# Differential attention: two units' half panels of queries and keys put behind the logits of one unit

## What is computed

```python
def diff_attention(h, pos, w_qkv, q_gain, k_gain, ..., rel_table, lam_init):
    qkv = h @ w_qkv
    q = rms_norm_2(qkv[..., :qk_w].reshape(b, s, DIFF_HEADS, 2, DIFF_QK_DIM), q_gain)
    k = rms_norm_2(qkv[..., qk_w:2 * qk_w].reshape(b, s, DIFF_HEADS, 2, DIFF_QK_DIM), k_gain)
    v = qkv[..., 2 * qk_w:].reshape(b, s, DIFF_HEADS, DIFF_V_DIM)
    ...
        sc = jnp.einsum('bqhcd,bkhcd->bhcqk', q_blk, k).astype(f32) * scale
        ...
        sc = jnp.where(causal_mask(i, s), sc + bias, NEG_INF)
        a = jax.nn.softmax(sc, axis=-1)
        wts = a[:, :, 0] - lam * a[:, :, 1]
        return jnp.einsum('bhqk,bkhv->bqhv', wts.astype(v.dtype), v)
    ...
    o = rms_norm_2(o, sub_gain) * (1.0 - lam_init)
    return o.reshape(b, s, DIFF_HEADS * DIFF_V_DIM) @ w_o
```

## Time and profile before

| | before |
|---|---|
| median of 3 runs | 2942.85 us (2942.21 to 2944.64) |
| the profiled execution | 2943.78 us |
| its span, first to last instruction | 2942.0 us |
| PE busy | 2830.5 us, 96% of the span |
| DVE busy | 1883.5 us, 64% |
| ACT busy | 1157.5 us, 39% |
| mean granted clock of PE | 0.989 of full speed |
| the loop over units, on PE | about 1468.8 to 1628 us of the span |

### The profile page before, as it was taken

One profiled execution on the slowest core, in us unless ns is written; L12 is line 12 of the kernel. 1 busy time (PEld: TensorE's weight loads), 2 busy tenths in 40 slices (PEclk: granted clock), 3 DMA queues, 4 the chain that ended last, 5 costly groups with the idle time before them and its releaser, 6 DMA issues.

```text
span 2942.0 us, 41954 instructions
## 1 busy us (share of the span) xinstructions
PE 2830.5 (96%) x14930; PEld 2267.2 (77%) x14930; DVE 1883.5 (64%) x3191; ACT 1157.5 (39%) x2228; POOL 726.7 (25%) x831
## 2 busy tenths in 40 slices
PE   8999999998999999999999899999989999999999
PEld 5777866776676899876766699987757767799987
DVE  6775346796345888447466688855755554788745
ACT  2111023333443566014255378711355551378501
POOL 1001003343141587000000078800000000188500
PEclk9999999999999999999999999999999999999999
DMA  4335422211112233322322123343211111233432
GB/s 154 109 105 119 131 92 80 79 65 65 47 50 83 79 102 105 113 90 103 101 85 70 58 86 109 103 131 93 86 43 36 37 37 66 71 101 109 138 98 93
DMA packets 81210, 259.15 MB, mean 88 GB/s; under 512 B 9128, under 2 KB 15656, under 8 KB 80776
## 3 DMA queue, kind: packets, MB, share of 16 engines
q1 hardware_dynamic: 64656, 227.64, 23.8%
q10 hardware_dynamic: 16376, 29.20, 3.4%
HBM read 242.51 MB, written 14.16 MB: 87 GB/s over the span
## 4 chain that ended last, share of the span: by engine, by line
PE 83%; DVE 10%; ACT 4%; issue 2%; POOL 1%; ACTq 0%; DMA 0%; SPq 0%; DVEq 0%
PE ps L327 17%; PE ps L328 16%; PE ps L329 16%; PE ps L1014 6%; PE ps L1015 6%; PE ps L1016 6%; PE ps L4381 1%; DVE w_lo L310 1%; PE ps L4426 1%; PE ps L4402 1%; PE ps L4403 1%; DVE w_hi L301 1%; PE ps L3896 1%; PE ps L1467 1%; PE ps L3156 1%
## 5 line engine op out<-in xcount | busy, mean ns | idle before, releaser
L301 DVE CAST w_hi<-raw 128x1024 fp32r<-128x1024 f32 (+1 forms) x311 | 212.2, 682 | 524.0 <-PE ps L329 492.7
L327 PE MATMUL ps<-xh,w_hi 128*128 128x512 f32 x1200 | 505.4, 421 | 32.1 <-DVE xl L851 12.3
L328 PE MATMUL ps<-xl,w_hi 128*128 128x512 f32 x1200 | 479.3, 399 | 0.0
L329 PE MATMUL ps<-xh,w_lo 128*128 128x512 f32 x1200 | 478.3, 399 | 0.0
L1376 POOL TENSOR_TENSOR w_lo<-raw,w_hi 128x256 fp32r<-128x256 f32 x440 | 337.0, 792 | 135.6 <-ACT w_hi L1067 132.7
L327 PEld LDWEIGHTS ps<-xh,w_hi 128*128 128x128 f32 x1200 | 228.1, 190 | 133.9 <-issue 43.8
L1368 POOL TENSOR_TENSOR raw<-raw 128x256 f32<-128x256 f32 x120 | 93.9, 803 | 952.7 <-DMA raw<-in_conv_up 904.8
L310 DVE TENSOR_TENSOR w_lo<-raw,w_hi 128x1024 fp32r<-128x1024 f32 (+2 forms) x259 | 308.6, 1191 | 12.4
L327 PE MATMUL ps<-ah,w_hi 128*128 128x512 f32 x704 | 278.5, 396 | 0.7 <-DVE w_lo L310 0.7
L329 PE MATMUL ps<-ah,w_lo 128*128 128x512 f32 x704 | 278.3, 395 | 0.0
L328 PE MATMUL ps<-al,w_hi 128*128 128x512 f32 x704 | 278.3, 395 | 0.0
(11 more groups left out here) (494 smaller groups left out, 5742.5 us busy)
## 6 DMA issues: line engine op xcount, KB each, us to landing
raw<-in_ffn_up SPq DMA_DIRECT2D x90, 512.0 KB, 3.5
raw<-in_conv_up SPq DMA_DIRECT2D x88, 512.0 KB, 3.4
raw<-in_ffn_down SPq DMA_DIRECT2D x32, 512.0 KB, 3.7
raw<-in_conv_down SPq DMA_DIRECT2D x32, 512.0 KB, 3.6
raw<-in_merge SPq DMA_DIRECT2D x24, 512.0 KB, 3.5
raw<-in_ple_gate SPq DMA_DIRECT2D x24, 512.0 KB, 3.4
raw<-in_diff SPq DMA_DIRECT2D x24, 512.0 KB, 3.4
raw<-in_mla SPq DMA_DIRECT2D x20, 512.0 KB, 3.4
```

Source lines behind the costliest of these rows:

```text
L301: dve.tensor_copy(self.w_hi[s][:, 0:n], self.raw[r][:, 0:n]).then_inc(self.sem["slot_hi"], 1)
L327: pe.matmul(out, wh, xh, start=start, stop=False)
L328: pe.matmul(out, wh, xl, start=False, stop=False)
L329: return pe.matmul(out, wl, xh, start=False, stop=stop)
```

## The change

Both halves of a panel are projected in the unit in which the first half stood, and the unit of the second half projects nothing. So whole panels of keys stand in the units with b = 0 and whole panels of queries in those with b = 2, behind the logits and the sum of that unit.

```diff
             item, half = self.item_in(u)
-            if item is not None:
-                self.project(pe, item, half)
+            if item is not None and half == 0:
+                self.project(pe, item, 0)
+                self.project(pe, item, 1)
             self.out.beside(pe, u)
```

## The result

The changed kernel takes 2969.98 us in the median of four runs (2968.68 to 2976.45), against 2942.94 us for the kernel before (2942.21 to 2944.64): a ratio of 1.0096, 95% interval 1.0084 to 1.0108. It is slower by 27.0 us; 30 us were forecast. The profiled execution took 2968.89 us, its span is 2967.1 us.

The account below looks back on a forecast made before the run. PE's own work was taken to bound the loop. Queries 16.8, keys 3.8 and clock 9.5 us sum to 30 us, set on the 2942.85 us median: 2973 us forecast, range 2961 to 2983.

Parts of the forecast that it names:

- The bound: In the loop, PE's own work sets the pace; any standstill adds time, and under 4 us could be won back.
- Queries, b = 3: At head borders, mask to next query sum stays 5.69 us; PE idles for the moved half, 6 x 2.8 = 16.8 us.
- Keys, b = 1: After b = 1's mask, the key sum waits for ACT's square: 2.3 us over six heads, 1.5 in the first, 3.8 together.
- The wait of 0.4 us: PE's wait before the key sum of b = 2, about 0.4 us in each of six heads.
- DVE's rounding ahead of the row minimum: In b = 2 the row minimum stands behind earlier rounding; PE's 5.6 us query panel covers this, so no cost.
- The clock: Idle of 3.3 us at five borders drops the clock: 1.9 us each, 9.5 us in all, bounds 0 and 16.
- the 1.9 us forecast for the first head: Idle stretch before the sum at the first head's border, 1.9 us, taken to cost the clock nothing.
- the two waits: PE's added waits for query sums (16.8 us) and key sums (3.8 us), leading to 2963 us without clock loss.
- the clock stays up: Rival: idle of 3.3 us at borders does not cost the clock, only the waits remain, 2963 us; chance 0.2.
- Long clock stretches at every border: Rival: each of six heads has 6.0 us at the lower clock, 37 us in sum, 2980 us; chance 0.08.
- the sum would no longer wait: Rival: at borders ACT squares before b = 3's exponentials, the waits vanish, up to 3.4 us faster, 2939 us; chance 0.06.

Follow-up runs that it names:

- the queries alone: Kernel before with only the query panels projected whole (b = 2), key panels split as before: 2972.71 us, ratio 1.0096.
- the shorter chain: Changed kernel with ACT's four bias DMA issues moved to the end of its work in b = 3: 2958.05 us, ratio 1.0046.
- The keys alone: Kernel before with only the key panels projected whole (b = 0), query panels split as before: 2945.50 us, ratio 1.0013.
- The filled kernel: Changed kernel with a useless half key panel ahead of the sum in b = 0 of heads 2 to 6: 2963.16 us, ratio 1.0065.
- the sum behind the panel: Changed kernel with each unit's sum behind its panel: 2952.43 us; also with ACT's copy ahead of the root in b = 0: 2951.33 us.
- the queries alone and the waits filled: Kernel before with only query panels whole, plus a useless half key panel ahead of the sum in b = 0 of heads 2 to 6: 2962.04 us.
- whole panels elsewhere: Changed kernel with whole panels behind the logits of b = 1 and b = 3 instead of b = 0 and 2: 2944.38 us, ratio 1.0006.
- the kernel before with the sum moved: Kernel before, halves as they were, with each unit's sum behind the half panel instead of ahead of it: 2939.03 us, ratio 0.9987.

## Why the prediction was right

**The bound.** PE set the pace, and what it stood still was added to the time. The waits in the rows grew by 16.1 us (from 3.2 to 18.1 + 1.2) and PE's idle time in the loop by 16.6 (from 163.76 - 157.56 = 6.2 to 190.19 - 167.40 = 22.8). The rest of the 26.4 us is busy time, 9.8 us more of it: 6.2 of this are the clock (below), and the other 3.6 are most likely waiting that falls inside a record: the next head's logits at the border shown (1540.82) last 0.73 us, and before 0.49 (1530.05). That DVE and ACT were idle for a third of the loop or more helped nothing, since the chain through them is a matter of order and not of their load.

**Queries, b = 3.** The step on which the forecast stood held to the hundredth: 5.69 us from mask to sum before and after, idle 3.17 us where 3.3 were worked out, a total wait of 18.1 us, 17.8 of it at the borders, where some 20 were named. The run with the queries alone and the one with the shorter chain show that it is this place and this chain.

**Keys, b = 1.** The part was right in kind and a little too large. In the head that ends at the border shown above, it is 2.55 us from mask to sum, and 2.65 were forecast:

```profile
1527.99 0.28 PE L3898 MATMUL ps<-maskc 128*128 128x128 bf16 x2
...
1529.91 0.57 ACT L3966 ACTIVATE tmp<-ps 128x512 f32<-128x512 f32 x1
...
1530.17 0.28 PE L3898 MATMUL ps<-maskc 128*128 128x128 bf16 x2
...
1530.54 1.12 PE L3881 MATMUL ps<-tmp,consts 128*128 128x512 f32 x2
```

The wait of 0.4 us that was to be seen before this sum is not among the waits; it shows only in the starts. The sum follows the logits' mask 0.37 us later (1530.17 to 1530.54), and where nothing held a sum the distance was 0.12, so some 0.25 us a head were lost where 0.4 were worked out. In the first head PE's wait came ahead of the logits, for the row minimum (0.62 us), and not ahead of the sum. That head became 4.15 us longer (1471.19 to 1493.15, before 1469.53 to 1487.34) where 2.8 + 1.5 = 4.3 were forecast. The keys alone cost 3.1 us, forecast 3.8. DVE's rounding ahead of the row minimum was covered, as said.

**The clock.** This term was too large: 9.5 us were taken, and the execution that was profiled lost 4 x 1.54 = 6.2. The rows of before gave a stretch of 3.4 or 6.0 us of work, and I took a value between; here all four were short ones, and one border kept the clock. That they were short is luck as far as the prediction goes: nothing in it told which would come, and with the six long ones of the queries alone the same waits would have given some 2979 us (an estimate: 2942.85 + 20.2 + 6 x 2.6). Nor did the length of the idle stretch decide. The trace of before, too, has half speed behind idle stretches of 1.74 us (ended at 1721.01) and 2.05 us (991.32), and none behind others of 1.7 us, so the 1.9 us forecast for the first head were no reason to put its clock at nothing, though it did hold there. Without the clock's 6.2 us the loop's 26.4 leave 20.2, and 20.6 had been worked out for the two waits. The filled kernel measures this split on its own: 6.8 us for the clock, 20.7 for the rest. The longest of the four executions, 2976.45 us, had a mean clock of 0.984 instead of 0.987 or 0.988, so the clock has a part in the spread of its runs. HAM oscillation, the section of the Trainium skill that the prediction cites (TensorE: Matmul & The Clock Gate), tells of a loop whose waits of some 3 to 5 us lost the clock in every turn. The trace agrees at four of the five long waits, of 3.2 to 3.3 us, and not at the fifth. Shorter waits than the section's lost it here as well: 1.82 us with the queries alone.

**The rivals.** That the clock stays up (2963 us) is refuted by the windows above; the filled kernel, whose clock does stay up, took 2963.16 us. Long clock stretches at every border (2980) did not come in the change, but came with the queries alone. That the sum would no longer wait, which would have ended on the other side, failed as expected: ACT's stream has the square where it had it. The runs with the sum behind the panel show that the rival's aim is within reach by another edit, but with whole panels new waits come up in the emptied units.

## What to carry to other kernels

Here a half panel was worth its 2.8 us beside another engine's chain, and moving it elsewhere in the same stream gave nothing back. Before moving such work on an in-order engine, measure the chain from its release to its end and see what is left beside it. Here even a panel that was ready earlier gained nothing, since the consumer's place in the other engine's order was not moved with it. A small reorder that puts a waiting instruction behind ready work may gain what gathering the work in one place loses.

## What was not expected of the hardware

The same idle stretch cost the clock differently: after 3.17 us (3.33 at the first of them) the granted clock fell to 0.50 for some 3.4 us behind four of five borders when a whole panel followed, and for 6.8 us behind each of the five, and behind the first border's 1.8 us too, with the queries alone, where half a panel followed. With the queries alone and the waits filled, that first border, left as it was, cost 3.4 us. The wait of 2.80 us at the loop's end is the same in all these kernels: the clock held behind it in the kernel before and in the change, was at 0.50 for 3.4 us with whole panels elsewhere, and for 6.8 us in the kernel before with the sum moved. So neither the length of the idle stretch nor what follows it settles the loss by itself, and what decides stays open. Filling the idle stretches with 60 useless matmuls made the kernel 6.8 us faster in one case and 10.7 us in the other.
